# Bias tables loaded by another queue, later waits in the expert retrieval, and half of the twelfth expert piece loaded ahead

## What is computed

```python
# first block, twice (layer 0: mLSTM + MoBA mixer, layer 1: differential attention)
x = x + g1 * mixer(rms_norm(x) * (1 + sc1) + sh1)
h = rms_norm(x) * (1 + sc2) + sh2
x = x + g2 * peer_ffn(h)         # 8 heads, top 16 of 128 x 128 product keys:
                                 # every token adds g_e * v_e * gelu(u_e . h) for 128 gathered rows
# second block, once: three attentions side by side
logits_na  = q k^T / 8 + rpb[dr, dc]        # neighbourhood, bias from a table
logits_dil = q k^T / 8 + t5[bucket(offset)] # dilated windows, bias from a table
logits_mem = q k^T / 8                      # against 256 memory rows
x = x + concat(out_na, out_dil, out_mem) @ w_out
# mixture of experts: 32 experts, top 2 within the best of 4 groups
x = x + sum over the 2 chosen e of gate_e * (silu(h w1[e]) * (h w3[e])) @ w2[e]
```

## Time and profile before

| | |
|---|---|
| median of 3 runs | 2306.08 us (2305.84 to 2307.43) |
| the profiled execution's own time | 2306.09 us |
| its span | 2304.3 us |
| PE busy, share of the span | 78% |
| DVE, ACT, POOL busy | 56%, 37%, 29% |
| moved by DMA | 920.49 MB, mean 399 GB/s |
| chain that ended last | DMA 48%, PE 32%, DVE 10%, ACT 6% |

### The profile page before, as it was taken

How to read it: one execution, slowest core, us unless ns; L and a number is a source line. 1 busy time by engine, 2 the same in 40 slices (tenths; PEclk the granted TensorE clock), 3 DMA queues, 4 the chain that set the end, 5 groups by cost and what they waited for, 6 DMA issues and landing times.

```text
span 2304.3 us, 30881 instructions
## 1 busy us (share of the span) xinstructions
PE 1789.9 (78%) x11196; PEld 848.4 (37%) x11196; DVE 1298.3 (56%) x3217; ACT 850.6 (37%) x2292; POOL 659.1 (29%) x606
## 2 busy tenths in 40 slices
PE   9999877695797777588779666877779997766666
PEld 4655521161352343153336112343327553222222
DVE  4878887668757766866776867555442331111111
ACT  1324354444445544454744435444333520000000
POOL 1002444434433433533443444333322300000000
PEclk9999887696798888689989667888979999788888
DMA  9988799999999999999999999999999399999998
GB/s 395 381 351 347 314 420 421 420 420 419 388 421 421 421 421 421 421 382 421 412 410 421 421 420 421 421 421 420 421 404 333 121 392 422 428 428 429 428 428 372
DMA packets 111150, 920.49 MB, mean 399 GB/s; under 512 B 12806, under 2 KB 15140, under 8 KB 19044
## 3 DMA queue, kind: packets, MB, share of 16 engines
q0 software_dynamic: 76800, 549.70, 57.9%
q1 hardware_dynamic: 34212, 369.02, 38.8%
HBM read 917.57 MB, written 6.06 MB: 401 GB/s over the span
## 4 chain that ended last, share of the span: by engine, by line
DMA 48%; PE 32%; DVE 10%; ACT 6%; issue 3%; POOL 1%; SPq 0%; DVEq 0%; POOLq 0%; ACTq 0%
DMA arena<-in_peer_uv_dram,arena 27%; DMA arena<-in_moe_pieces_dram 14%; PE summed L1560 8%; DVE y_g L3153 4%; PE gp L1652 3%; PE gp L1105 3%; DMA mod<-in_w_parts_dram 3%; DMA arena<-in_w_slots_dram 2%; PE gp L1967 2%; PE gp L1110 2%; PE gp L1648 2%; DMA arena<-in_w_parts_dram 1%; PE gp L1781 1%; ACT arena L2311 1%; PE gp L1532 1%
## 5 line engine op out<-in xcount | busy, mean ns | idle before, releaser
L1560 PE MATMUL summed<-arena 64*64 64x512 f32 x4096 | 693.8, 773 | 338.5 <-ACT arena L2311 313.9
L3153 DVE CUSTOM_DVE_ANT_0 y_g<-arena,h 128x1024 f32<-128x1024 f32 x512 | 627.3, 1225 | 389.6 <-DMA arena<-in_peer_uv_dram,arena 332.1
L1036 POOL DMA_INDIRECT arena<-in_peer_uv_dram,arena x512 | 592.8, 1158 | 885.9 <-PE summed L1560 805.4
L1560 PEld LDWEIGHTS summed<-arena 64*64 64x64 f32 x4096 | 136.3, 157 | 760.3 <-ACT arena L2311 660.3
L2305 ACT ACTIVATE arena<-arena 128x1 f32<-128x1 f32 x512 | 102.7, 201 | 558.0 <-DVE arena L3153 556.9
L1967 PE MATMUL gp<-arena,mod 128*32 128x512 f32 x1008 | 156.5, 758 | 98.5 <-DMA arena<-in_moe_pieces_dram 98.5
L2311 ACT ACTIVATE arena<-cst,arena 128x128 f32<-128x128 f32 x512 | 205.5, 401 | 16.8
L3546 DVE TENSOR_TENSOR mod<-mod,gp 128x512 f32<-128x512 f32 x8 | 5.5, 687 | 353.7 <-ACT mod L2620 353.7
L2308 ACT ACTIVATE arena<-arena 128x1 f32<-128x1 f32 x512 | 150.8, 294 | 16.6
L1967 PEld LDWEIGHTS gp<-arena,mod 128*32 128x32 f32 x1008 | 31.7, 124 | 214.8 <-DMA arena<-in_moe_pieces_dram 156.8
L2620 ACT ACTIVATE mod<-gp 128x512 f32<-128x512 f32 x8 | 4.8, 597 | 246.7 <-PE gp L1967 246.7
(11 more groups left out here) (530 smaller groups left out, 2339.3 us busy)
## 6 DMA issues: line engine op xcount, KB each, us to landing
arena<-in_moe_pieces_dram SPq DMA_DIRECT2D x92, 2048.0 KB, 25.5
arena<-in_w_slots_dram SPq DMA_DIRECT2D x43, 2048.0 KB, 12.5
arena<-in_w_parts_dram SPq DMA_DIRECT2D x42, 1024.0 KB, 9.3
mod<-in_w_parts_dram SPq DMA_DIRECT2D x23, 1024.0 KB, 9.6
arena<-in_peer_uv_dram,arena POOLq DMA_INDIRECT x512, 15.7
t_rep<-t_rows POOLq DMA_DIRECT2D x1, 3066.0 KB, 18.3
arena<-t_rep POOLq DMA_DIRECT2D x1, 2304.0 KB, 12.8
ext<-in_w_parts_dram SPq DMA_DIRECT2D x2, 1024.0 KB, 22.8
```

The source lines that it names most:

```text
L1036: pool.indirect_dma_start(rowbuf[b], None, a["peer_uv"].rearrange("l n d -> (l n) d"), bass.IndirectOffsetOnAxis(ap=idx[:, col(n):col(n) + ...
L1560: mm = pe.matmul(op[o:o + HALF, b, :], diag[i:i + HALF, n % DIAGS, i:i + HALF], rowbuf[n % ROWS][i:i + HALF, D + b * 512:D + (b + 1) * 512 ...
L3153: v.tensor_tensor_reduce(y[:, t, :], rowbuf[n % ROWS][:, 0:D], h[:, t, :], 1.0, 0.0, ALU.mult, ALU.add, dots[:, c:c + 1]).then_inc(udot, 1)
```

## The change

The bias tables are loaded by SP, behind its first four weight slices and before the fifth; DVE masks them as the first thing of `last_attention`. In `second_layer` three waits on `d_hT` move from the step of the transposes to that of the first reader. In the experts' stage `hT` is no longer filled on the usual path; the overflow path fills it itself, for both tiles. The first half of piece 11 goes there, ahead; only its second half waits for `p_used` and slot 0. ACT gets one tiny square root behind the last row.

```diff
@@ sync
             for n in range(phase_slots["in2"][0], phase_slots["in2"][0] + RING):
                 sync.wait_ge(vsum, rows_left(place[n]))
                 sync.dma_start(ring[:, place[n], :], a["w_slots"][n]).then_inc(w_landed[place[n]], 16)
+            sync.wait_ge(bias_w, 64)
+            sync.wait_ge(x_ready, 4 * T + 1)
+
+            sync.dma_start(dil_bias, bass.AP(tensor=t5_rep.tensor, offset=127,
+                                             ap=[[12 * TW - 1, P], [TW, 12], [1, 384]])).then_inc(loaded, 16)
...
+            for hh in range(NA_HEADS):
+                for r2 in range(2):
+                    sync.dma_start(na_bias[r2 * GRID_W:(r2 + 1) * GRID_W, hh, :].rearrange("p (j n) -> p j n", j=6),
...
             for n in range(phase_slots["in2"][0] + RING, len(slots)):
                 load_weights(n)
@@ sync, experts
             sync.wait_ge(r_mm, T)
+            sync.dma_start(flat_hT, a["moe_pieces"][0, AHEAD][:, 0:8 * S]).then_inc(p_in[AHEAD - 1], 16)
             sync.wait_ge(y_ready, 3)
             sync.wait_ge(h_ready, 5 * T + 5)
             first_bits(9, (1, 2))
             first_bits(10, (1, 2))
             for n in range(AHEAD, PIECES):
                 sync.wait_ge(p_used, n - AHEAD + 1)
-                next_piece(0, n)
+                r = piece_place(0, n)
+                sync.dma_start(moe_slot[r][:, 8 * S:], a["moe_pieces"][0, n][:, 8 * S:]).then_inc(p_in[r], 16)
@@ gpsimd: the 17 bias loads and their wait count are gone
             pool.wait_ge(x_ready, 4 * T + 1)
-
-            pool.dma_start(dil_bias, bass.AP(tensor=t5_rep.tensor, offset=127,
...
             load_gain(5, a["g_ffn_2"][0])
             divide_last()
@@ tensor, second_layer
                     if s == 5:
                         pe.wait_ge(d_h, 2 * t + 1)
                         turn_tile(h, t)
+                    if s == 9:
                         pe.wait_ge(d_hT, 6 * t + 2)
...
                     if s == 64:
                         pe.wait_ge(d_y, t + 1)
                         turn_tile(y, t)
+                    if s == 67:
                         pe.wait_ge(d_hT, 6 * t + 4)
...
                         turn_tile(h, t)
+                    if s == 84:
                         pe.wait_ge(d_hT, 6 * t + 6)
@@ tensor, experts
             pe.wait_ge(h_ready, 5 * T + 7)
-            turn_scaled(0)
-            turn_scaled(1)
             keep_clock("out2", 2, h[:, 0, 0:CH])
...
                     pe.wait_ge(p_in[r], piece_landed(p, 8 + b))
+                    if first(p) and 8 + b == AHEAD:
+                        pe.wait_ge(p_in[AHEAD - 1], piece_landed(p, AHEAD - 1))
@@ scalar
             rows_to(PICKS)
+            act.activation(small[:, 16:17], eps[:, 0:1], ACT.Sqrt)
             half_square(1, 0, x_ready, 4 * T)
...
-            act.wait_ge(r_mm, T)
-            for b in range(2):
-                move_half(b, sp_[:, b, :])
-
@@ vector
             def mask_tables():
-                v.wait_ge(bias_in, 16 * (NA_HEADS + 17))
+                v.wait_ge(loaded, 16 * (NLOADS + 20))
...
             def last_attention():
+                mask_tables()
                 head_inverse("block2", 0)
                 head_scale("block2", 0)
                 head_scale("block2", 1)
                 head_inverse("block2", 1)
-                mask_tables()
```

More of the change, by code:

```diff
@@ L726, in program @@
         moe_slot = [ring[:, place[n], :] for n in last_held] + [zbuf[:, 0:4096], tk[:, 0:4096], arena[:, 28672:32768], y_g2[:, :]]
+        flat_hT = hT[:, :, :].rearrange("p k n -> p (k n)")
         def down_piece(q, n):
@@ L732, in down_piece @@
                 return lambda e, f: quarters[4 * e + f]
+            if isinstance(q, int) and q == 0 and n == AHEAD:
+                split = [flat_hT[:, c:c + S] for c in range(0, 8 * S, S)]
+                split += [moe_slot[piece_place(q, n)][:, c:c + S] for c in range(8 * S, 16 * S, S)]
+                return lambda e, f: split[4 * e + f]
             w = moe_slot[piece_place(q, n)].rearrange("p (e f c) -> p e f c", e=QUAD, f=4)
@@ L789, in piece_landed @@
             if isinstance(q, int) and q == 0 and n < AHEAD:
-                return 16 if n not in BITS else 16 * sum(len(bits) for bits in BITS.values())
+                return 16 if n not in BITS else 16 * (1 + sum(len(bits) for bits in BITS.values()))
             return q * 32 + 16 * (2 + (n - AHEAD) // MOE_RING)
@@ L873, in _ @@
                 sync.dma_start(ring[:, place[n], :], a["w_slots"][n]).then_inc(w_landed[place[n]], 16)
+            sync.wait_ge(bias_w, 64)
+            sync.wait_ge(x_ready, 4 * T + 1)
+            sync.dma_start(dil_bias, bass.AP(tensor=t5_rep.tensor, offset=127,
+                                             ap=[[12 * TW - 1, P], [TW, 12], [1, 384]])).then_inc(loaded, 16)
+            W = NA_HEADS * NDR * RW
+            for hh in range(NA_HEADS):
+                for r2 in range(2):
+                    sync.dma_start(na_bias[r2 * GRID_W:(r2 + 1) * GRID_W, hh, :].rearrange("p (j n) -> p j n", j=6),
+                                   bass.AP(tensor=na_rep.tensor,
+                                           offset=hh * NDR * RW + (1 - r2) * RW + GRID_W - 1,
+                                           ap=[[W - 1, GRID_W], [RW, 6], [1, GRID_W]])).then_inc(loaded, 16)
             for n in range(phase_slots["in2"][0] + RING, len(slots)):
@@ L1194, in turn_plain, with turn_scaled @@
                 turned[0] += 1
-            def turn_scaled(b):
+            def turn_scaled(t, b):
                 n = turned[0]
@@ L1200, in turn_scaled @@
                     k = 4 * b + c
-                    mm = pe.transpose(sp_[:, b, c * P:(c + 1) * P], h[:, 1, k * P:(k + 1) * P], ident)
+                    mm = pe.transpose((gp, sp_)[t][:, b, c * P:(c + 1) * P], h[:, t, k * P:(k + 1) * P], ident)
                 mm.then_inc(turn_done, 1)
@@ L2046, in _ @@
                 pe.wait_ge(down_moved, QUADS + 3)
+                for t in range(T):
+                    for b in range(2):
+                        turn_scaled(t, b)
                 hT_ready()
@@ L2467, in half_square, with move_half @@
                                accum_out=small[:, 46 + b:47 + b]).then_inc(sumsq, 1)
-            def move_half(b, bank):
+            def move_half(b, bank, t=1):
                 act.wait_ge(turn_done, turned[0] + 1)
-                act.activation(hT[:, 4 * b:4 * b + 4, P:S], bank.rearrange("p (c n) -> p c n", c=4), ACT.Copy).then_inc(turn_moved, 1)
+                act.activation(hT[:, 4 * b:4 * b + 4, t * P:(t + 1) * P], bank.rearrange("p (c n) -> p c n", c=4), ACT.Copy).then_inc(turn_moved, 1)
                 turned[0] += 1
@@ L2657, in _ @@
             with act.If(act.value_load(flag[0:1, 0:1], min_val=0, max_val=2 * S) > 0):
+                for t in range(T):
+                    for b in range(2):
+                        move_half(b, (gp, sp_)[t][:, b, :], t)
                 expert(0, 0)
```

## The result

The changed kernel takes 2313.26 us (median of 8 runs, 2309.47 to 2317.78) against 2307.26 us of the kernel before in the same runs (8 runs, 2305.84 to 2310.8): a ratio of 1.0027, 95% interval 1.0018 to 1.0037. The forecast was 2301.6 us, with 2306.5 us as the upper end. The profiled execution took 2312.15 us with a span of 2310.3 us, 6.0 us more than the span before.

The account below looks back on a forecast made before the run. DMA engines were taken to bound the gather and experts' stages, with PE between; waits gave -4.0 and -0.5 us, all else 0, so 2306.09 became 2301.6 us, range 2298 to 2306.5.

Parts of the forecast that it names:

- The bias tables: Projection before the last attention: tables on SP's queue cost 0, the fifth weight slice landing at 1743.7, before PE needs it.
- stall = 15 c - 9.3: PE's stall in us at the fifth weight slice, if each of 15 small table pieces takes c us.
- Rival D: Tables much slower in q1 than in q0, stalling PE beyond the gain: 2314.8 us at 1.5 us a piece; chance 0.08.
- Rival A: The fifth weight slice is late and PE stands still 2.3 us: 2303.9 us; chance 0.17.
- The waits on d_hT: Row gathers: earlier sums fill idle DMA time, 4.0 us gained behind s = 5 of both tiles, 0.5 at s = 64.
- Rival C: PE's pace behind s = 9 gives back the gathers' gain, leaving 1.2 us: 2304.9 us; chance 0.19.
- Half of piece 11: Experts' start: fills 1.9 us of DMA idleness, but PE limits round 0, so 0 gained.
- the transposes left out: Before the gather of tokens: PE waits for DVE's selection matrix anyway, so 0 gained.
- the square root: Behind the last row: Sqrt table loaded 1.3 us earlier, covered by PE's first slice, so 0; without cover 1.3 us gained.
- Rival B: The half piece pays as well, if PE ends round 0 earlier: -2.2 us, 2299.4 us; chance 0.14.
- The fear of a fall of the clock at the gather of tokens: Experts' first gather of tokens: longer PE idleness without the transposes might drop its clock and cost 2.6 us; put at 0.
- Tables earlier: Last attention: earlier tables and the masks' new place give 0, since PE works without a gap before the first scores.

Follow-up runs that it names:

- e1: The kernel before with only the three waits on d_hT moved: 2308.08 us, ratio 1.0001 to the kernel before.
- e2: The kernel before with only the bias tables loaded by SyncE and masked first: 2314.14 us, ratio 1.0028.
- e8: The kernel before with dil_bias alone moved to SyncE, the 16 small pieces still on GpSimd: 2307.71 us, ratio 1.0006.
- e3: The kernel before with only the experts' part: half of piece 11 ahead, no transposes and copies on the usual path: 2307.70 us, ratio 1.0003.
- e5: The kernel before with 8 more transposes on PE at s = 5 in both tiles, ahead of the counted ones: 2307.08 us, ratio 1.0007.
- e10: The changed kernel with the 16 small table pieces shared, heads 0 to 3 by SyncE, 4 to 7 by GpSimd: 2312.41 us, ratio 1.0021.

## Why the prediction was wrong, by its own steps

The sum was -4.5 us for the waits and 0 for everything else. By e1 the waits gave nothing that could be measured, and by e2 the tables cost 6 us; both steps failed, and the second alone gives the sign.

**The bias tables: the step that failed.** It read "Either way SP is done by 1729.2". The cost of SyncE's seventeen issues was taken as their bare length, 5.6 to 11.6 us; they took 24.2. The bare length was right: from 1734 on they go at 0.63 us each, 0.67 with the gap. Missing was that an issue of many small runs is held while those ahead wait for the slices. The row for it was in hand: GpSimd's five pieces with "13.87 <-issue" ahead of them, a like hold on the other engine, where nothing urgent stood behind it (e8 shows GpSimd held 10 to 13 us after every five such pieces, so what holds it need not be the same). On SyncE the weight slices stand behind it. Worked out with the 13.87 us, SyncE would have been done at 1743 at the latest, and the stall would have stood in the sum.

How much of the 3.83 us is the hold, and how much the tables' bytes ahead of the slice, no run separates. An estimate: from 1730 to 1735 the DMA share of the changed kernel is 0.81, from 1735 to 1740 it is 0.73, so the engines idled 0.95 + 1.35 = 2.3 us while SyncE was still issuing. Had all pieces stood in the queue, the slice could have come at most about that much sooner; some 1.5 us of the wait would then be the bytes. The prediction had `dil_bias` and the first piece through at 1729.8 and the rest at 1736.9; measured, the last packet of `dil_bias` starts at 1733.2 and the last of the small ones at 1743.4.

**The price of a small piece** in the DMA engines was not the error. In the changed kernel from 1734 to 1740 q1's packets took

```profile
q1 hardware_dynamic: 3335, 0.82, 70.5%
```

so 0.705 x 6 us for 0.82 MB / 98304 bytes = 8.3 pieces: 0.51 us each, near the 0.47 us taken. With this the rule of thumb "stall = 15 c - 9.3" gave no stall; what it left out was the time until the slice is issued, and that the engines wait for pieces that SyncE has not issued yet. Rival D named the right place and sign and the wrong mechanism, and its price would not have come from 0.51 us. Rival A's stall of 2.3 us was 3.8, and it went with 1.6 us more of slow matmuls: behind the 3.83 us in which PE stood still the granted clock of the next 4 us reads 0.58, which is the lower level of 1.2 GHz for most of them.

```profile
1749.00:1753.00 4.00, 4.00 (x22) 4.00 (x23) 0.59 (x1) 0.00 (x0) 0.00 (x0) 0.58 1.02 438
```

**The waits on d_hT: the step that failed** was "Each is less than the idle time behind it, so I take both whole". The term of 4.0 us, and the 0.5 us at s = 64, measured 0 (e1: -2.8 to +3.2 us by its interval; by the stretch in the traces 0.4 us longer on average with the waits moved). PE's sums and the gathers came earlier by even more than forecast (3.6 and 5.4 us at the parts, of which 1.1 and 1.5 us were there before), and the dips emptied; the reckoning of idle time was that of the mean over 16 engines, where a row waits for the last of them, and the packets behind took longer. Rival C had the sign, but not for its reason, the pace of PE behind s = 9.

**Half of piece 11, the transposes left out, the square root:** 0 was forecast, and no run shows another number; for the first two e3 holds it to -1.6 to +3.2 us. Rival B didn't come. The fear of a fall of the clock at the gather of tokens pointed at a thing that is there (5.4 us in place of 3.84). It comes with the transposes too (e1), but in one of five traces, and without them in five of seven, so this term, put at 0, may be a microsecond too low. The square root wasn't tried alone; the stretch from the last row sum to PE's first scores behind the fourth slice is 33.1 to 34.2 us in the six traces without it and 33.5 to 34.3 us in the six with it, and the 1.3 us that it would have gained without cover are not seen.

**Tables earlier: 0 gained,** as forecast for this trace. In other executions with the tables on GpSimd, DVE had them later: in e5 it waited 6.16 us for them and PE then 2.09 us for DVE. That is the little that an earlier place could win, and it lies below what the medians here can show.

## What to carry to other kernels

An issue is not free because its queue's engine is idle: before a batch of small-run DMAs is put ahead of something urgent in the same engine's list, look in the trace for that kind of DMA being held in its issue ("<-issue" gaps on the engine that has them now), and count that hold as a delay for all that stands behind it. Idle DMA time, when it is a mean over 16 engines, can be worth nothing: in the dip looked at here the last engine never ran dry. Look at windows of 1 us inside a dip, and follow one transfer from issue to use. And test each part of a bundle by itself: here one part lost 6 us, and the others together moved the time by less than could be measured.

## What was unexpected in the hardware

- One issue of 384 runs of 256 bytes took between 0.63 us and 9.09 us on SyncE in the changed kernel, and 10.94 us in e10, by what was waiting ahead of it; 1536 runs of 384 values could be issued in 0.38 us just before.
- With two queues at work the engines served 285 packets of one against 286 of the other, whatever their size: 1.31 MB against 0.10 MB in 4 us.
- GpSimd sends the 256-byte runs of the tables in packets of mean 2 KB (720 for 1.48 MB), SyncE in single runs (3335 for 0.82 MB).
- GpSimd is held 10 to 13 us after every five issues of 384 runs, with nothing else in its queue (e8).
- Executions differ by 4 us in when they come to the rows (the dot product of row 101 at 517.0 to 521.0 us over twelve traces), nearly all of it from the first 250 us, which no kernel here changes.
